# Another order for the last, narrow chunk of a dense SwiGLU block: gate piece in two halves, up piece ahead of the down pieces

## The reference

```
x = x + m                                  # residual after attention
h = rmsnorm(x, norm_ffn[0])
f = (silu(h @ wg) * (h @ wu)) @ wd         # wg, wu: 1024 x 2816, wd: 2816 x 1024
x = x + f
h = rmsnorm(x, norm_mix[1])                # head of the LRU block
```

## Time and profile before

| | us |
|---|---|
| median of 3 runs | 1418.39 (1415.43 to 1418.74) |
| the profiled execution: its time | 1418.9 |
| the profiled execution: its span, first to last instruction | 1417.1 |
| TensorE busy | 1384.8 (98% of the span) |
| VectorE busy | 1122.1 (79%) |
| ScalarE busy | 935.1 (66%) |
| mean granted TensorE clock | 0.988 of full speed |

### The profile page before, as it was taken

The page is one execution under the profiler, slowest core; times in us unless marked ns, Lnnn a source line. Parts: engine busy times, 40 slices in busy tenths (PEclk is TensorE's granted clock), DMA queues, the critical chain, the costliest instruction groups (busy, mean ns, idle before and its releaser), DMA issues.

```text
span 1417.1 us, 18318 instructions
## 1 busy us (share of the span) xinstructions
PE 1384.8 (98%) x6814; PEld 1165.7 (82%) x6814; DVE 1122.1 (79%) x972; ACT 935.1 (66%) x736; POOL 50.2 (4%) x69
## 2 busy tenths in 40 slices
PE   8999999999989999999999999999999999999996
PEld 8987888879978888888888888888888888888885
DVE  5666554457677899888988989888898898988886
ACT  6655443346746777777776867777777686777764
POOL 4000000000000000000000000000000000000000
PEclk9999999999997999999999999999999999999998
DMA  9544654843375999999999999999999999999991
GB/s 315 168 143 155 211 199 155 259 148 119 120 288 217 327 384 369 388 392 362 376 388 409 339 382 402 351 383 390 363 371 389 411 336 395 393 353 379 390 374 69
DMA packets 147117, 437.84 MB, mean 309 GB/s; under 512 B 7225, under 2 KB 30386, under 8 KB 147074
## 3 DMA queue, kind: packets, MB, share of 16 engines
q1 hardware_dynamic: 143264, 424.96, 80.0%
q0 software_dynamic: 3744, 12.28, 3.0%
q10 hardware_dynamic: 66, 0.02, 0.0%
HBM read 429.35 MB, written 7.88 MB: 309 GB/s over the span
## 4 chain that ended last, share of the span: by engine, by line
PE 92%; DVE 5%; ACT 2%; issue 1%; DMA 0%; DVEq 0%; SPq 0%; ACTq 0%
PE ps L1345 86%; PE ps L1743 2%; DVE w_lo L1230 1%; ACT w_hi L470 1%; PE ps L1788 0%; PE ps L1614 0%; DMA w_ring<-in_attn_w_qkv_dram 0%; PE ps L1675 0%; DVE w_lo L811 0%; DVE work L1104 0%; PE ps L1439 0%; PE ps L1560 0%; ACT work L685 0%; DVE hn L841 0%; PE ps L1691 0%
## 5 line engine op out<-in xcount | busy, mean ns | idle before, releaser
L470 ACT ACTIVATE w_hi<-w_ring 128x2048 fp32r<-128x2048 f32 (+1 forms) x257 | 487.6, 1909 | 183.5 <-PE ps L1345 173.1
L1230 DVE TENSOR_TENSOR w_lo<-w_ring,w_hi 128x2048 fp32r<-128x2048 f32 x191 | 434.1, 2288 | 71.0 <-ACT w_hi L470 71.0
L1345 PE MATMUL ps<-w_hi,xt_hi 128*128 128x512 f32 (+1 forms) x1152 | 450.9, 391 | 2.2 <-DVE xt_lo L856 1.5
L1345 PE MATMUL ps<-w_lo,xt_hi 128*128 128x512 f32 (+1 forms) x1152 | 446.2, 387 | 0.0
L1345 PE MATMUL ps<-w_hi,xt_lo 128*128 128x512 f32 (+1 forms) x1152 | 445.9, 387 | 0.0
L1345 PE MATMUL ps<-w_hi,split 128*128 128x512 f32 x1152 | 358.8, 393 | 7.4 <-DVE split L1114 4.1
L470 ACT ACTIVATE w_hi<-work 128x2048 fp32r<-128x2048 f32 x144 | 275.3, 1917 | 114.2 <-PE ps L1345 114.2
L1230 DVE TENSOR_TENSOR w_lo<-work,w_hi 128x2048 fp32r<-128x2048 f32 x141 | 320.9, 2288 | 35.0 <-ACT w_hi L470 34.3
L1345 PEld LDWEIGHTS ps<-w_hi,split 128*128 128x128 f32 x1152 | 216.1, 189 | 55.6 <-issue 7.9
L1345 PEld LDWEIGHTS ps<-w_hi,xt_hi 128*128 128x128 f32 x1152 | 217.1, 188 | 46.2 <-DVE xt_lo L856 1.9
L1345 PEld LDWEIGHTS ps<-w_lo,xt_hi 128*128 128x128 f32 x1152 | 216.8, 188 | 44.6
(11 more groups left out here) (265 smaller groups left out, 687.7 us busy)
## 6 DMA issues: line engine op xcount, KB each, us to landing
w_ring<-in_moe_w_up_dram SPq DMA_DIRECT2D x72, 1024.0 KB, 8.2
w_ring<-in_moe_w_down_dram SPq DMA_DIRECT2D x72, 1024.0 KB, 6.0
work<-in_moe_w_gate_dram SPq DMA_DIRECT2D x64, 1024.0 KB, 7.4
w_ring<-in_moe_w_gate_dram SPq DMA_DIRECT2D x48, 1024.0 KB, 7.1
work<-in_moe_w_up_dram SPq DMA_DIRECT2D x40, 1024.0 KB, 7.9
work<-in_moe_w_down_dram SPq DMA_DIRECT2D x40, 1024.0 KB, 6.2
w_ring<-in_attn_w_qkv_dram SPq DMA_DIRECT2D x11, 1024.0 KB, 11.2
w_ring<-in_ffn_w_gate_dram SPq DMA_DIRECT2D x11, 1024.0 KB, 5.1
```

The lines of the kernel that those rows point to most:

```text
L470: return nc.scalar.activation(out, in_, ACT.Copy)
L1230: V.tensor_tensor(w_lo[:, half_slot(n), :], land(n), w_hi[:, half_slot(n), :].bitcast(F32), ALU.subtract).then_inc(lo_ready, 1)
L1345: ins = T.matmul(acc, stationary, moving, start=start and k == 0, stop=stop and k == 2)
```

## The change

The pieces of the last chunk are numbered anew: gate 44, up 45, the two down pieces of chunk 4 46 and 47, the chunk's own down piece 48. TensorE does half of the gate piece, the transposes of chunk 4, the other half, waits for `fl`, does the up piece, the first down piece of chunk 4, the transposes of chunk 5, the second down piece of chunk 4, waits for `fl`, and does down piece 48. ScalarE makes the high part of piece 50 behind the copies of chunk 5, not ahead of them; VectorE makes the low part of piece 48 behind the product of chunk 5 and that of piece 49 behind the subtractions of chunk 5. No instruction that computes is added or removed.

```diff
-    static += [cols8(fg, CW * FC)] + [rows2(fd, CW * (FC - 1) + 256 * h) for h in range(2)]
-    static += [cols8(fu, CW * FC), rows2(fd, CW * FC)]
+    static += [cols8(fg, CW * FC), cols8(fu, CW * FC)]
+    static += [rows2(fd, CW * (FC - 1) + 256 * h) for h in range(2)] + [rows2(fd, CW * FC)]
...
-        return P_FFN + 2 if i == 0 else f_gate_at(i) + (4 if i < FC else 3)
+        return P_FFN + 2 if i == 0 else f_gate_at(i) + (4 if i < FC else 1)
...
-        return f_gate_at(i + 1) + (2 if i + 1 < FC else 1) if i < FC else f_up_at(FC) + 1
+        return f_gate_at(i + 1) + 2 if i < FC else f_up_at(FC) + 3
@@ ScalarE
-                hi_upto(f_gate_at(i) + (2 if last else 3))
+                hi_upto(f_gate_at(i) + 3)
...
-            hi_upto(P_IN + 1)
+            hi_upto(P_IN)
             aT_split_hi(2 * FC, 2)
             aT_split_hi(2 * FC + 1, 2)
+            hi_upto(P_IN + 1)
@@ VectorE
+            lo_upto(P_IN - 1)
             aT_split_lo(2 * FC, 2)
             aT_split_lo(2 * FC + 1, 2)
             lo_upto(P_IN + 1)
@@ TensorE
-            def narrow(n, banks):
+            def narrow(n, banks, cs=range(KC)):
...
-                for c in range(KC):
+                for c in cs:
...
-                ins.then_inc(piece_used, 1)
+                if KC - 1 in cs:
+                    ins.then_inc(piece_used, 1)
...
                 if last:
-                    narrow(f_gate_at(i), (0, 1))
+                    narrow(f_gate_at(i), (0, 1), range(KC // 2))
                     turn_chunk(i - 1, 4)
+                    narrow(f_gate_at(i), (0, 1), range(KC // 2, KC))
+                    pe.wait_ge(fl, 2 * i)
+                    narrow(f_up_at(i), (2, 3))
...
                     for h in range(2):
+                        if last and h:
+                            turn_chunk(FC, 2)
                         down(f_down_at(i - 1) + h, (4, 5, 6, 7), aT_hi, aT_lo, (2 * h, 2 * h + 1), i == 1 and h == 0, False)
-                if last:
-                    narrow(f_up_at(i), (2, 3))
-                else:
+                if not last:
...
-            turn_chunk(FC, 2)
             pe.wait_ge(fl, 2 * FC + 2)
```

## The result

The changed kernel takes 1409.76 us (median of 5 runs, 1407.98 to 1411.0), the kernel before 1416.52 (5 runs, the three known ones and two new). The ratio is 0.9942, with a 95% interval of 0.9915 to 0.997. The forecast of 1414.5 and its range of 1411.2 to 1418.2 were both too high. The profiled execution of the changed kernel has a span of 1406.1 against 1417.1: 11.0 us, where the plan had 3.9.

What follows compares the result with a forecast made beforehand. The prediction took TensorE's own instructions, 92% of the chain, to bound the kernel. Gaps of 2.00, 0.56 and 1.32 us, together 3.88, taken as 3.9, came off the median 1418.39, giving 1414.5 us; range 1411.2 to 1418.2.

Steps and rivals of the forecast that it cites:

- The three gaps: TensorE's waits behind chunk 4's transposes (2.00 us), up piece 47 (0.56) and chunk 5's transposes (1.32) vanish, together 3.88 us.
- The last down piece: Sign in the last chunk: down piece 48 should start at 305.9 us and not at 309.74.
- the LRU's first transposes: Sign behind the last chunk: these transposes should start at about 315.8 us.
- The thin cover: Second half of the gate piece, 2.88 us, hides chunk 4's copy and subtractions with 1.2 us to spare.
- one cover fails: Rival: the half gate piece doesn't hide the splits, some or all of the first gap returns, 1416.5 us; chance 0.10.
- The moved parts of pieces: High and low parts moved on ScalarE and VectorE in the last chunk cost nothing, 0.3 us at the most.
- The first square: ScalarE, behind the last chunk: wanted at 309.7 us, 3.77 after the down piece's start; tight, but a slip costs nothing.
- The gain given back later: Rival: LRU and experts start earlier but wait longer for something timed on its own, 1418.4 us; chance 0.10.
- The clock: Rival: low-clock spells behind TensorE's stalls change; slower, 1422.3 us, chance 0.07, or faster, 1411.1 us, chance 0.08.
- the first spell: Granted clock of 0.69 over 390 to 401 us, 3.4 us of full-speed time lost; without it 1411.1 us.
- Both spells: Clock of 0.69 over 390 to 401 us and 0.54 over 430 to 447, losing 3.4 and 7.8 us.
- What was quoted and not used: Rule on TensorE's clock: activity windows don't start with the kernel, so the shift itself decides nothing, either direction can come.

Runs made afterwards that it cites:

- turn_last: The changed kernel with the transposes of chunk 5 put behind both down pieces of chunk 4; ratio to the kernel before 0.9974.
- before_again: The kernel before, run again with no edit; 12 runs from 1413.15 to 1423.64 us, ratio 1.0007.
- warm_lru: The changed kernel with 16 further unread matmuls where TensorE waits for the recurrence at the end of the LRU; median 1413.49 us, ratio to the kernel before 0.9973.
- warm_both: The changed kernel with 16 unread matmuls added at the LRU's wait and 18 for 8, 5 for 3 at the routing's; median 1412.24 us, ratio 0.9966.

## Why the prediction was wrong, point by point

- **The three gaps, 2.00 + 0.56 + 1.32 us: right.** They are gone from the chain, and the block is 3.99 us shorter against 3.88 to 3.9 said. The last down piece starts at about 305.7 (half of the 10.95 us behind 300.20; said 305.9), the LRU's first transposes at 315.39 (said 315.8). Taken by parts the halves give 1.85 (said 2.00) and the order 2.15 (said 1.88).
- **The thin cover: right.** VectorE was idle for 0.33 us ahead of the subtractions of chunk 4 (said 0.34), so the low part of piece 46 was in no one's way, and the up piece follows without a wait. The rival "one cover fails" did not come about.
- **The moved parts of pieces: right, with little to spare.** VectorE waited 1.50 us for the first bank, so the adds weren't held up. The first square was said to be tight, wanted 3.77 us behind the start of the down piece. It started at 309.17, some 3.5 behind, directly after the table load and a square root of one column, as these rows of ScalarE show, without an idle time of its own:

```profile
309.02 0.20 ACT L484 ACTIVATE small<-small 128x1 f32<-128x1 f32 x1
309.17 1.06 ACT L496 ACTIVATE hn<-xres 128x1024 f32<-128x1024 f32 x1
```

  The second add, for which it waits, ends at 308.45 + 0.69 = 309.14, so nothing was lost. What the prediction did not see is that this cover hangs on the place of the transposes (turn_last).
- **The gain given back later: did not happen.** The starts of the LRU's projections are 322.10 and 317.76, 4.34 us apart, the same as at the last add (315.51 and 311.17); and over whole runs, at equal clock, the 4.0 us are still there at the end.
- **The clock: the step that failed.** The sum took 3.9 us off 1418.39 and let the lost clock stay what it was, a change of nothing. The prediction had the rival and its direction ("without the first spell it would be 3.4 less"), but took it for an outside chance of 0.08, let only the first spell go in this direction, and rested the lower end of the range on it. Measured, the five runs of the changed kernel lost 11.0 us of clock on average, where the kernel before loses 15.4 over its 111 runs: 4.4 us, close to the 4.7 by which the forecast was missed. Their time without it is 1398.5, and the forecast in these terms would have been 1402.5 - 3.9 = 1398.6. Both spells move from run to run, and the kernel before ranges over 13 us, not over the 3.3 that three runs show. With lost clocks of 10 to 21 us a median of five runs can lie 2 us or more off its centre, on either side and in each of the two kernels. In the first comparison it fell in favour of the change: 6.8 us between the medians, of which 4.1 are the change's. Over all jobs the difference of the means is 5.4, with an uncertainty of 0.8 (4.8 without the first five runs), and that of the times without lost clock 4.1. The range should have gone down to about 1408.
- **What stays open.** That the first five runs were luck is the best reading, not a shown one. Of the 24 later runs of the changed kernel only 8 are as short as the longest of those five, 1411.0. If runs were independent, a median as low as 1409.76 would come in about 15 of 100 sets of five, but five out of five at 1411.0 or less in fewer than 1 of 100. Something about that job may have favoured the clock; no run here tells.
- **A source of spread that neither the prediction nor the theories name: the start of the kernel.** The first 144 matmuls, by the chain of waits of the kernel before and of before_again:

```profile
13.43 17.67 PE ps L1345 x144
```
```profile
13.32 19.00 PE ps L1345 x144
```

  The clock over the first 20 us is 1.00 in the one and 0.91 in the other. The chain begins with the first weight load. It takes 7.67 us (warm_lru) to 9.72 (warm_both) in the twelve profiles whose chain begins with the same load (that of the kernel before begins with another), these matmuls start between 12.69 and 14.74, and the products of chunk 4 between 281.56 and 286.04 us. A load that is late counts as no lost clock, so it is part of the scatter in the time without it.
- **What was quoted and not used.** The Trainium skill (TensorE: Matmul & The Clock Gate, Part 1: The HAM clock gate) says that the same kernel changes its clock at other moments from run to run. The rows agree: the kernel before has 0.83 and 0.76 in one profile and 0.91 and 0.90 in the next over the same stretches. The prediction quoted the rule and did not use it for the range. The Trainium skill (the same title, HAM oscillation — how this bites in real kernels) advises to keep TensorE free of long gaps. Here the filling at the routing narrowed the spread from 10.4 to 2.6 us, that at the LRU alone did not (9.5), and neither brought a gain clear of the noise.

## What to carry to other kernels

When the chain of waits shows small gaps on TensorE between stretches of its own work, their sum is a good forecast of what a reordering brings (3.88 said, 3.99 measured), provided the half piece put in as cover is longer than the work that it hides, and provided that what is moved out of the way on the other engines isn't moved in front of the next thing that the chain needs. Before giving a range for a change of 0.3%, find out what one kernel does from run to run: read its mean granted clock in each run and compare times with the lost clock taken off, or compare only runs of equal clock. That holds between kernels that do the same work in their waits: filling a wait lowered the lost clock here (15.8 to 10.1 us) with no gain in time clear of the noise. A difference in clock between two profiles is no property of the change until the unchanged kernel has failed to show it.

## What the runs showed of the hardware that was not expected

- The same kernel on one core takes 1411.6 to 1424.6 us, 0.9%, with mean clocks of 0.993 to 0.985; without the lost clock the medians of the kernel before in three jobs are 1402.4, 1402.6 and 1402.5.
- The clock can fall behind quite short stalls: in the profile with the halved gate piece alone it did so behind gaps of 0.56 and 1.3 us (7.39 us for 24 matmuls, against 5.75) that had left it at 1.00 in both profiles of the kernel before.
- Unread matmuls in a wait lower the lost clock (15.8 to 10.1 us with both waits filled) without a gain in time that is clear of the noise. A low spell costs only where TensorE is on the chain (10.28 us with it, 10.27 without, over the routing), and the fillers themselves run slowly once the clock has fallen (7.07 us for 18, where 18 took 4.08 at the full clock).
- The first weight load takes 7.67 to 9.72 us in twelve profiles, and the first large group of matmuls starts 2.9 us behind its end in each (13.06 and 10.17 in the changed kernel, 14.74 and 11.85 in warm_both).
